# Token stacks by whole 128x128 transposes, with a new order of the mixer's instructions

## Chip, core and metric

One core of a Trainium2 chip. The metric is the device time of one launch in microseconds (us); the median of a few runs counts.

## What is computed

A decoder trunk of two layers for 256 tokens of width 2048, in float32. Each layer is RMS norm, one input projection, three parallel mixers (HGRN2, latent attention with 8 heads, RWKV-7 with 8 heads of 64), their outputs joined and projected, a residual, then norm and a SwiGLU feed-forward. The parts that matter here, cut from the reference:

```python
# attention of one block of 128 queries
s = where(k_idx <= q_idx, (q_nope @ k_nope.T + q_rope @ k_rope.T) * scale, MASK)
p = softmax(s);  o = p @ v
# RWKV-7, per head and token
sa    = state @ -kk_t
state = state * w_t + outer(sa, kk_t * a_t) + outer(v_t, k_t)
y_t   = state @ r_t
```

## The kernel before

The weights (some 400 MB) stream through four slots of `raw`. ScalarE rounds each half slot to `w_hi` (line 450), VectorE takes the rest as `w_lo` (line 875), and TensorE does three products of 128x128 by 128x512 for each tile (lines 1447 to 1449). This fills nearly all of the time. Between the input projection and the output projection of each layer lies the mixer stretch (TensorE from line 1760 on), in which attention and RWKV-7 are worked off together. Its order is written out by hand, once for each engine: lines 688 to 772 for ScalarE, 1203 to 1320 for VectorE, the end of the GpSimd block for GpSimd, lines 1799 to 1937 for TensorE. Engines meet by semaphores only, and each works its list in order.

RWKV-7 is evaluated in chunks of 64 tokens. `rw_r`, `rw_k`, `rw_v`, `rw_a` and `rw_kk` are held as 4 pairs of heads by 256 tokens, two heads of 64 channels in the halves of the 128 partitions. 16 tiles of 64x64 for each half (`JC` = 16) stand for 4 pairs by 4 chunks (`NC` = 4).
- `q_norm` scales the query's rotary part, on which GpSimd then does six rotary steps (lines 420 to 426). `k_sums`, `k_norm`, `up`, `q_turn`, `k_turn`, `r_turn` prepare the attention's keys and queries. `up(5)` to `up(7)` are the last products of the up projection; ScalarE squares and copies them in `up_out`.
- `product(left, right)` makes 16 tiles for each half by 32 products of 64x64 (`both_heads`, line 1736). The first one, of `kk` and `a`, gives the matrix of which a unit triangular inverse is wanted. VectorE masks each product (`product(k, dst, ...)`, line 1257): `mab`, `mak_t`, `mrk_t`, `mrb_t`.
- The inverse starts on VectorE from 2x2 pairs (lines 1282, 1283 and the block transposes at line 1262). Five levels follow. For each one GpSimd masks `mab` into `rw_level` (line 434), `level_g(k)` multiplies it with `inv_t`, ScalarE evicts that (`gt_out`, line 685), `level_x(k)` multiplies with `inv`, and VectorE's `level(k)` subtracts and turns (lines 1270, 1262), each in two halves.
- `stack(z, bank)` brings the tokens of `v`, `a` and `k` onto the partitions, chunk by chunk, by 32 products of 64x64 with the unit matrix; ScalarE evicts the result in one piece (`stacked`, line 671) to `v_st`, `b_st`, `k_st`.
- `attend(p)` makes the scores of a pair of heads, `score_max(p)` on VectorE adds the mask (line 1173), takes maxima (line 1176) and two small products (line 1180), `softmax(p)` on ScalarE the exponentials, `probs(p)` on VectorE scales by the inverse sums in two instructions (line 1192), `p_turn(p)` turns them, `probs_out(p)` evicts them, `mix(hf)` multiplies with the values; `mix_out` and `mix_lo` split the result for the output projection.
- In the recurrence TensorE goes over the four chunks (lines 1905 to 1937) with small products (`each`, line 1889), VectorE scales the right side (line 1313) and the state (line 1317), ScalarE copies `sa` (line 770).

PSUM has eight banks; `stack` of `v` and `a` uses 0 and 1, the products 2 and 3, later 4 to 7.

Of the kernel before, what the change touches and what calls it, by code (L numbers as in the profile page):

```python
# [35 lines left out]
P = 128  # L36
D = 2048
SEQ = 256
TT = SEQ // P
# [14 lines left out]
RC = 64  # L54
# [58 lines left out]
def build(nc, stream, x_in, positions, params, consts, lora, gains, rows, out):  # L113
    with ExitStack() as ctx:
# [237 lines left out]
        def _(pool):  # L352
# [24 lines left out]
            for l in range(DEPTH):  # L377
# [53 lines left out]
                for k in range(len(RW_LEVELS)):  # L431
                    if k:
                        pool.wait_ge(S("rw_gt_mm"), 10 * l + 2 * k)
                    tt(rw_level, mab, lev_lo[:, k, :].unsqueeze(1).broadcast_to([P, JC, RC]), ALU.mult).then_inc(
                        S("rw_level_ready"), 1)
# [4 lines left out]
        def _(act):  # L440
# [66 lines left out]
            for l in range(DEPTH):  # L507
# [160 lines left out]
                def stacked(k, dst, b0):  # L668

                    act.wait_ge(S("rw_stack_mm"), 3 * l + k + 1)  # L670
                    nc.scalar.activation(dst.rearrange("p n f -> p (n f)"), bank(b0, 2), ACT.Copy).then_inc(
                        S("rw_stacked"), 1)
# [62 lines left out]
                nc.scalar.activation(srw[:, 48:64], srw[:, 32:48], ACT.Exp, scale=-C0).then_inc(S("rw_half_decay"), 1)  # L735
                up_out(5)
                q_out(1)
                k_std(0)
                stacked(0, v_st, 0)
# [15 lines left out]
                softmax(3)  # L755
# [4 lines left out]
                probs_out(3)  # L760
                mix_out(0)
                gt_out(3)
                mix_out(1)
# [3 lines left out]
                stacked(2, k_st, 6)  # L767
# [76 lines left out]
        def _(dve):  # L844
# [108 lines left out]
            for l in range(DEPTH):  # L953
# [216 lines left out]
                def score_max(p):  # L1170
# [3 lines left out]
                       "mla_s_read", 4 * l + p + 1)  # L1174
                    for off, cols, n in parts:
# [8 lines left out]
                def probs(p):  # L1184
# [5 lines left out]
                    for off, cols, n in parts:  # L1190
                        z = scores[:, h2, cols]
                        u(tt(z, z, along(small[:, 64 + off + 2 * p:66 + off + 2 * p], n), MUL))  # L1192
# [46 lines left out]
                dve.sem_inc(S("rw_v_ready"), 1)  # L1239
                v(tt(rw_a, rw_a, rw_kk, MUL))  # L1240
                q_norm()
                dve.wait_ge(S("rw_exp"), 3 * l + 1)
                v(tt(rw_r, rw_r, rw_e_r, MUL))
                k_sums(0)
                dve.wait_ge(S("rw_exp"), 3 * l + 2)
                v(tt(rw_kk, rw_kk, rw_e_kk, MUL))
                k_norm(0)
                dve.wait_ge(S("rw_bonus_mm"), ev)
                v(tt(rw_bonus.rearrange(flat), bank(2, 2), rw_v.rearrange(flat), MUL))
                dve.wait_ge(S("rw_exp"), 3 * ev)  # L1250
                vs(tt(rw_a, rw_a, rw_e_b, MUL), "rw_b_done", ev)
                vs(tt(rw_k, rw_k, rw_e_b, MUL), "rw_ab_done", ev)
                k_sums(1)

# [26 lines left out]
                product(1, mab, 2, "strict_lo")  # L1281
                v(tt(inv, mab, over(C("pair_lo"), JC, RC), MUL))
# [3 lines left out]
                dve.sem_inc(S("rw_xt"), 1)  # L1286
                k_norm(1)
                dve.wait_ge(S("rw_half_decay"), ev)
                hd = srw[:, 48:64].rearrange("p (j c) -> p j c", j=4)
                md = srw[:, 64:80].rearrange("p (j c) -> p j c", j=4)  # L1290
                v(tt(md[:, :, 0:3], hd[:, :, 0:3], hd[:, :, 1:4], MUL))
                score_max(0)
                level(0)
                score_max(1)
                probs(0)
                score_max(2)
                probs(1)
                score_max(3)
                level(1)
                probs(2)  # L1300
                probs(3)
                level(2)
                mix_lo(0)
                mix_lo(1)
                product(2, mak_t, 4, "strict_up")
                level(3)
                product(3, mrk_t, 6, "incl_up")
                product(4, mrb_t, 4, "incl_up")
# [119 lines left out]
        def _(pe):  # L1428
# [81 lines left out]
            for l in range(DEPTH):  # L1510
# [245 lines left out]
                def unit_of(hp, n):  # L1756
                    return idst[hp, :]

                def stack(z, b0):
                    both_heads(b0, range(JC), chunk_of(z), unit_of, RC).then_inc(S("rw_stack_mm"), 1)  # L1760
# [347 lines left out]
```

## Time and profile before

| | us |
|---|---|
| median of 3 runs (2363.12 to 2363.3) | 2363.16 |
| profiled run | 2363.51 |
| its span, first to last instruction | 2361.7 |
| TensorE busy | 2329.8 (99%) |
| VectorE busy | 1331.0 (56%) |
| ScalarE busy | 1090.3 (46%) |
| GpSimd busy | 60.6 (3%) |

A matmul's busy time overlaps with the next one's, so the start of one row to the start of the next is its cost. In a chain of waits each step goes back to what released it. An instruction's row also holds time in which it has begun but is held up.

### The profile page before, as it was taken

To read this page: it belongs to the slowest core of one execution; us is meant where nothing else is said; L and a number is where in the kernel's file an instruction comes from. 1 tells how busy PE (TensorE), PEld (TensorE's weight loads), DVE (VectorE), ACT (ScalarE), POOL (GpSimd) and SP (SyncE) were. 2 spreads that over 40 slices of the span, in tenths; PEclk is the share of its full clock that TensorE was granted. 3 is DMA by queue.
4 is the path that set the end of the run, shared out by engine and by line. 5 is a ranking of instruction groups with operands and counts; after the bars stand their busy time and mean duration, and the time that the engine had idled before them with its cause. 6 is when DMAs were issued, how large, how long until landed. Compare 5 with 4: busy or idle time off the path is not lost.

```text
span 2361.7 us, 34240 instructions
## 1 busy us (share of the span) xinstructions
PE 2329.8 (99%) x13929; PEld 1931.9 (82%) x13929; DVE 1331.0 (56%) x1402; ACT 1090.3 (46%) x1336; POOL 60.6 (3%) x60
## 2 busy tenths in 40 slices
PE   8999999999999999999999999999999999999999
PEld 7888688888888888888888886888888888888887
DVE  5686676544545445455556857665454554454444
ACT  6554644444443344444445546455444433444443
POOL 0000210000000000000000002100000000000000
PEclk9999999999999999999999999999999999999999
DMA  7453304555555555555554532045555555555553
GB/s 297 165 185 134 115 18 164 193 181 194 191 182 196 192 190 189 195 183 191 186 189 152 196 113 102 21 165 190 183 192 195 179 195 196 192 185 193 189 187 141
DMA packets 59523, 407.11 MB, mean 172 GB/s; under 512 B 6608, under 2 KB 6704, under 8 KB 13200
## 3 DMA queue, kind: packets, MB, share of 16 engines
q1 hardware_dynamic: 58720, 401.66, 47.4%
q0 software_dynamic: 688, 3.78, 0.5%
q8 instruction: 88, 1.44, 0.2%
q14 instruction: 27, 0.22, 0.0%
HBM read 403.32 MB, written 2.10 MB: 172 GB/s over the span
## 4 chain that ended last, share of the span: by engine, by line
PE 94%; DVE 5%; issue 1%; ACT 0%; DMA 0%; DVEq 0%; SPq 0%; ACTq 0%
PE psum L1447 28%; PE psum L1449 28%; PE psum L1448 28%; PE psum L1641 2%; PE psum L1889 1%; PE psum L1736 1%; PE psum L1976 1%; PE psum L1542 1%; PE psum L1481 1%; DVE arena L1192 1%; DVE arena L1262 0%; DVE small L1176 0%; DVE arena L1173 0%; PE psum L1717 0%; DVE arena L1283 0%
## 5 line engine op out<-in xcount | busy, mean ns | idle before, releaser
L875 DVE TENSOR_TENSOR w_lo<-raw,w_hi 128x1024 fp32r<-128x1024 f32 (+2 forms) x752 | 901.5, 1205 | 848.7 <-ACT w_hi L450 841.8
L450 ACT ACTIVATE w_hi<-raw 128x1024 fp32r<-128x1024 f32 (+2 forms) x752 | 781.9, 1044 | 1082.6 <-PE psum L1449 1081.0
L1447 PE MATMUL psum<-w_hi,hT_hi 128*128 128x512 f32 (+2 forms) x2128 | 821.6, 386 | 3.1 <-DVE w_lo L875 3.1
L1449 PE MATMUL psum<-w_hi,hT_lo 128*128 128x512 f32 (+2 forms) x2128 | 816.4, 384 | 0.0
L1448 PE MATMUL psum<-w_lo,hT_hi 128*128 128x512 f32 (+2 forms) x2128 | 816.3, 384 | 0.0
L1447 PEld LDWEIGHTS psum<-w_hi,hT_hi 128*128 128x128 f32 x2128 | 399.8, 188 | 81.7 <-DVE w_lo L875 2.4
L1449 PEld LDWEIGHTS psum<-w_hi,hT_lo 128*128 128x128 f32 x2128 | 399.7, 188 | 78.3
L1448 PEld LDWEIGHTS psum<-w_lo,hT_hi 128*128 128x128 f32 x2128 | 399.9, 188 | 76.5
L1447 PE MATMUL psum<-w_hi,act_hi 128*128 128x512 f32 x872 | 340.4, 390 | 0.0
L1449 PE MATMUL psum<-w_hi,act_lo 128*128 128x512 f32 x872 | 339.4, 389 | 0.0
L1448 PE MATMUL psum<-w_lo,act_hi 128*128 128x512 f32 x872 | 339.3, 389 | 0.0
L1449 PEld LDWEIGHTS psum<-w_hi,act_lo 128*128 128x128 f32 x872 | 163.7, 188 | 34.0
L1447 PEld LDWEIGHTS psum<-w_hi,act_hi 128*128 128x128 f32 x872 | 163.7, 188 | 33.6
L1448 PEld LDWEIGHTS psum<-w_lo,act_hi 128*128 128x128 f32 x872 | 163.7, 188 | 33.6
L1641 PE MATMUL psum<-raw,arena 128*128 128x384 f32 (+1 forms) x192 | 71.8, 525 | 2.0 <-ACT arena L639 1.3
L1641 PEld LDWEIGHTS psum<-raw,arena 128*128 128x128 f32 x192 | 35.4, 190 | 31.1 <-issue 13.8
L1382 DVE TENSOR_TENSOR act_lo<-psum,act_hi 128x1024 f32 (+1 forms) x22 | 26.9, 1224 | 37.9 <-ACT act_hi L825 37.9
L887 DVE SCALAR_TENSOR_TENSOR hT_lo<-psum,gain_col,hT_hi 128x256 fp32r<-128x256 f32 x64 | 26.6, 477 | 13.7 <-ACT hT_hi L472 13.7
L1736 PE MATMUL psum<-arena 64*64 64x64 f32 x1024 | 32.4, 219 | 1.5 <-ACT arena L685 1.5
L1736 PEld LDWEIGHTS psum<-arena 64*64 64x64 f32 x1024 | 30.8, 135 | 3.4 <-ACT arena L685 1.8
L825 ACT ACTIVATE act_hi<-psum 128x1024 f32 (+1 forms) x22 | 22.6, 1027 | 20.8 <-PE psum L1976 20.8
L908 DVE TENSOR_TENSOR x<-x,psum 128x1024 f32<-128x1024 f32 x23 | 27.9, 1213 | 4.9 <-PE psum L1449 4.9
(317 smaller groups left out, 1206.9 us busy)
## 6 DMA issues: line engine op xcount, KB each, us to landing
raw<-stream_dram SPq DMA_DIRECT2D x360, 1024.0 KB, 4.8
raw<-stream_dram SPq DMA_DIRECT2D x16, 512.0 KB, 3.5
raw<-stream_dram SPq DMA_DIRECT2D x8, 768.0 KB, 4.2
raw<-stream_dram SPq DMA_DIRECT2D x8, 640.0 KB, 3.7
x<-x_in_dram SPq DMA_DIRECT2D x4, 512.0 KB, 9.2
lor<-lora_dram POOLq DMA_DIRECT2D x2, 832.0 KB, 10.6
con<-consts_dram POOLq DMA_DIRECT2D x1, 1648.0 KB, 12.1
out_dram<-x SPq DMA_DIRECT2D x3, 512.0 KB, 7.4
```

The costliest lines, as they stand in the source:

```text
L450: nc.scalar.activation(w_hi[:, q % HALF_RING, 0:2 * w], raw[:, j % 4, hf * 2 * w:(hf + 1) * 2 * w], ACT.Copy).then_inc(hi_done, 1)
L875: tt(w_lo[:, q % HALF_RING, 0:2 * w], raw[:, j % 4, hf * 2 * w:(hf + 1) * 2 * w], w_hi[:, q % HALF_RING, 0:2 * w].bitcast(F32), SUB).then_ ...
L887: last = stt(hT_lo[:, 4 * c + k, :], bank(x_turn_bank(n, c), 2)[:, k * SEQ:(k + 1) * SEQ], gain_col[:, n * KT + 4 * c + k:n * KT + 4 * c + ...
L908: vs(tt(xs, xs, psum[:, b0:b0 + 2, :], ADD), "x_added", n_added)
L1192: u(tt(z, z, along(small[:, 64 + off + 2 * p:66 + off + 2 * p], n), MUL))
L1382: tt(act_lo[:, k, :], bank(4, 2).rearrange("p (k t) -> p k t", k=4), act_hi[:, k, :].bitcast(F32), SUB).then_inc(S("act_lo_ready"), 1)
L1447: mm(o, a_hi, w_hi[:, r, cols], start=(k == 0), stop=False)
L1448: mm(o, a_hi, w_lo[:, r, cols], start=False, stop=False)
L1449: last = mm(o, a_lo, w_hi[:, r, cols], start=False, stop=(k == n_k - 1))
L1481: last = tr(bank(x_turn_bank(n, c), 2)[:, k * SEQ + t * P:k * SEQ + (t + 1) * P], x[:, t, c * CH + k * P:c * CH + (k + 1) * P], ident)
L1641: last = mm(psum[:, UP_BANK[c] + t, 0:w], src[:, k, t * P:(t + 1) * P], raw[:, c % 4, k * w:(k + 1) * w], start=(k == 0), stop=(k == nk - 1))
L1736: last = mm(bank(b0, 2)[hp, m * w:(m + 1) * w], left(hp, n), right(hp, n), start=True, stop=True)
```

## The change

`stack` now turns a whole block of 128 channels by 128 tokens with one transpose, eight in all. The result has tokens on the partitions and two heads side by side in the columns, so `stacked` puts each of the four combinations of token half and head into its place by an eviction of its own, two of which go from one half of the partitions to the other. The orders on all four engines change: the product of `kk` and `a` is ahead of `k_turn(0)`, `r_turn` and the stack of `a`; the first inverse and the mask of level 0 are taken by VectorE right from PSUM, and `mab` is written later; `score_max` is divided into `score_add` and the rest; `probs` scales in four instructions with a column of scalars; `softmax(3)`, `p_turn(3)`, `probs(3)`, `level_x(3)`, `level(3)`, the stack of `k` and the last product move. The diff, cut to its core:

```diff
     pool.wait_ge(S("rw_m_ready"), 4 * l + 1)
-    for k in range(len(RW_LEVELS)):
-        if k:
-            pool.wait_ge(S("rw_gt_mm"), 10 * l + 2 * k)
+    for k in range(1, len(RW_LEVELS)):
+        pool.wait_ge(S("rw_gt_mm"), 10 * l + 2 * k)
         tt(rw_level, mab, lev_lo[:, k, :].unsqueeze(1).broadcast_to([P, JC, RC]), ALU.mult).then_inc(
...
         act.wait_ge(S("rw_stack_mm"), 3 * l + k + 1)
-        nc.scalar.activation(dst.rearrange("p n f -> p (n f)"), bank(b0, 2), ACT.Copy).then_inc(
-            S("rw_stacked"), 1)
+        turned = bank(b0, 2).rearrange("p (m h i) -> p m h i", h=2, i=RC)
+        tiles = dst.rearrange("p (m c) i -> p m c i", c=2)
+        halves = (EVEN, ODD)
+        for h in range(2):
+            for c in range(2):
+                last = nc.scalar.activation(tiles[halves[h], :, c, :], turned[halves[c], :, h, :], ACT.Copy)
+        last.then_inc(S("rw_stacked"), 1)
...
     nc.scalar.activation(srw[:, 48:64], srw[:, 32:48], ACT.Exp, scale=-C0).then_inc(S("rw_half_decay"), 1)
+    q_out(1)
+    stacked(0, v_st, 0)
     up_out(5)
-    q_out(1)
     k_std(0)
-    stacked(0, v_st, 0)
     up_out(6)
...
     softmax(2)
-    softmax(3)
     probs_out(0)
...
     probs_out(2)
-    probs_out(3)
+    softmax(3)
     mix_out(0)
     gt_out(3)
+    probs_out(3)
     mix_out(1)
...
     gt_out(4)
-    stacked(2, k_st, 6)
+    stacked(2, k_st, 4)
     for c in range(NC):
...
-    def score_max(p):
+    def score_add(p):
         h2, b0 = slice(2 * p, 2 * p + 2), 4 + 2 * (p % 2)
...
+    def score_max(p):
+        h2 = slice(2 * p, 2 * p + 2)
         for off, cols, n in parts:
...
         settle()
-        for off, cols, n in parts:
-            z = scores[:, h2, cols]
-            u(tt(z, z, along(small[:, 64 + off + 2 * p:66 + off + 2 * p], n), MUL))
+        for h in range(2 * p, 2 * p + 2):
+            for off, cols, n in parts:
+                z = scores[:, h, cols]
+                u(ts(z, z, small[:, 64 + off + h:65 + off + h], None, MUL))
         settle()
...
         v(tt(rw_v, v_first[:, :, :], rw_v, SUB))
-    dve.sem_inc(S("rw_v_ready"), 1)
+        dve.sem_inc(S("rw_v_ready"), 1)
+    q_norm()
     v(tt(rw_a, rw_a, rw_kk, MUL))
-    q_norm()
     dve.wait_ge(S("rw_exp"), 3 * l + 1)
     v(tt(rw_r, rw_r, rw_e_r, MUL))
-    k_sums(0)
     dve.wait_ge(S("rw_exp"), 3 * l + 2)
     v(tt(rw_kk, rw_kk, rw_e_kk, MUL))
+    dve.wait_ge(S("rw_exp"), 3 * ev)
+    v(tt(rw_a, rw_a, rw_e_b, MUL))
+    k_sums(0)
+    dve.wait_ge(S("rw_bonus_mm"), ev)
+    vs(tt(rw_bonus.rearrange(flat), bank(2, 2), rw_v.rearrange(flat), MUL), "rw_bonus_done", ev)
     k_norm(0)
-    dve.wait_ge(S("rw_bonus_mm"), ev)
-    v(tt(rw_bonus.rearrange(flat), bank(2, 2), rw_v.rearrange(flat), MUL))
-    dve.wait_ge(S("rw_exp"), 3 * ev)
-    vs(tt(rw_a, rw_a, rw_e_b, MUL), "rw_b_done", ev)
-    vs(tt(rw_k, rw_k, rw_e_b, MUL), "rw_ab_done", ev)
     k_sums(1)
+    dve.wait_ge(S("rw_half_decay"), ev)
+    hd = srw[:, 48:64].rearrange("p (j c) -> p j c", j=4)
+    md = srw[:, 64:80].rearrange("p (j c) -> p j c", j=4)
+    v(tt(md[:, :, 0:3], hd[:, :, 0:3], hd[:, :, 1:4], MUL))
...
-    product(1, mab, 2, "strict_lo")
-    v(tt(inv, mab, over(C("pair_lo"), JC, RC), MUL))
+    dve.wait_ge(S("rw_m_mm"), 4 * l + 1)
+    v(tt(inv, bank(2, 2).rearrange("p (n t) -> p n t", n=JC), over(C("pair_lo"), JC, RC), MUL))
     vs(stt(inv, inv, -1.0, over(idst, JC, RC), MUL, ADD), "rw_x", 10 * l + 1)
...
     dve.sem_inc(S("rw_xt"), 1)
+    dve.wait_ge(S("mla_rope_done"), ev)
+    v(tt(rw_level, bank(2, 2).rearrange("p (n t) -> p n t", n=JC), over(lev_lo[:, 0, :], JC, RC), MUL))
+    dve.sem_inc(S("rw_level_ready"), 1)
+    vs(tt(rw_k, rw_k, rw_e_b, MUL), "rw_ab_done", ev)
     k_norm(1)
-    dve.wait_ge(S("rw_half_decay"), ev)
-    hd = srw[:, 48:64].rearrange("p (j c) -> p j c", j=4)
-    md = srw[:, 64:80].rearrange("p (j c) -> p j c", j=4)
-    v(tt(md[:, :, 0:3], hd[:, :, 0:3], hd[:, :, 1:4], MUL))
+    product(1, mab, 2, "strict_lo")
+    score_add(0)
     score_max(0)
     level(0)
+    score_add(1)
     score_max(1)
     probs(0)
+    score_add(2)
     score_max(2)
+    score_add(3)
     probs(1)
-    score_max(3)
     level(1)
     probs(2)
+    score_max(3)
+    level(2)
     probs(3)
-    level(2)
     mix_lo(0)
     mix_lo(1)
+    level(3)
     product(2, mak_t, 4, "strict_up")
-    level(3)
     product(3, mrk_t, 6, "incl_up")
-    product(4, mrb_t, 4, "incl_up")
+    product(4, mrb_t, 6, "incl_up")
     level(4)
...
-    def unit_of(hp, n):
-        return idst[hp, :]
...
     def stack(z, b0):
-        both_heads(b0, range(JC), chunk_of(z), unit_of, RC).then_inc(S("rw_stack_mm"), 1)
+        for j in range(4):
+            for t in range(TT):
+                last = tr(bank(b0, 2)[:, (TT * j + t) * P:(TT * j + t + 1) * P], z[:, j, t * P:(t + 1) * P], ident)
+        last.then_inc(S("rw_stack_mm"), 1)
...
             pe.wait_ge(S("rw_x"), 10 * l + 2 * k + hf + 1)
+            if k == 0:
+                pe.wait_ge(S("rw_m_ready"), 4 * l + 1)
             if not last:
...
     if l == 0:
-        pe.wait_ge(S("rw_v_ready"), ev)
+        pe.wait_ge(S("rw_shifted"), 4 * l + 3)
         stack(rw_v, 0)
-    up(5)
     pe.wait_ge(S("rw_rk"), ev)
...
     if l:
-        pe.wait_ge(S("rw_v_ready"), ev)
+        pe.wait_ge(S("rw_v_ready"), l)
         stack(rw_v, 0)
+    up(5)
     up(6)
     up(7)
+    pe.wait_ge(S("rw_bonus_done"), ev)
+    product(rw_kk, rw_a, 2)
     k_turn(0)
-    pe.wait_ge(S("rw_b_done"), ev)
-    product(rw_kk, rw_a, 2)
+    r_turn(range(4))
+    r_turn([4])
     pe.wait_ge(S("rw_stacked"), 3 * l + 1)
     stack(rw_a, 0)
-    r_turn(range(4))
-    r_turn([4])
     attend(0)
...
     level_g(2)
+    p_turn(2)
     level_x(2)
-    p_turn(2)
-    p_turn(3)
     mix(0)
     level_g(3)
+    p_turn(3)
+    level_x(3)
     mix(1)
...
     product(rw_k, rw_kk, 4)
-    level_x(3)
+    level_g(4)
     pe.wait_ge(S("mla_mix_lo"), 2 * ev)
     product(rw_k, rw_r, 6)
-    level_g(4)
     pe.wait_ge(S("rw_m_ready"), 4 * l + 2)
-    product(rw_a, rw_r, 4)
+    stack(rw_k, 4)
     pe.wait_ge(S("rw_m_ready"), 4 * l + 3)
-    stack(rw_k, 6)
+    product(rw_a, rw_r, 6)
     level_x(4)
...
         if c == 0:
-            pe.wait_ge(S("rw_stacked"), 3 * ev)
+            pe.wait_ge(S("rw_m_ready"), 4 * ev)
+            each(6, 0, stacked(mrk_t, 0), stacked(v_st, 0), first=True)
             pe.wait_ge(S("rw_xt"), 12 * ev)
-        if c < NC - 1:
+        elif c < NC - 1:
             each(2, 0, stacked(k_st, c), stacked(v_st, c), first=True)
-            if c:
-                each(2, 0, unit, old)
+            each(2, 0, unit, old)
         pe.wait_ge(S("rw_rhs_ready"), NC * l + c + 1)
...
         if c == 0:
-            pe.wait_ge(S("rw_m_ready"), 4 * ev)
-        each(6, 256 * c, stacked(mrk_t, c), stacked(v_st, c), first=True)
-        if c:
+            pe.wait_ge(S("rw_stacked"), 3 * ev)
+            each(2, 0, stacked(k_st, 0), stacked(v_st, 0), first=True)
+        else:
+            each(6, 256 * c, stacked(mrk_t, c), stacked(v_st, c), first=True)
             each(6, 256 * c, in_chunk(rw_r, c), old)
...
```

## Rows read from the trace of the kernel before

**Rows 1.** Page, part 4: the chain that ended last, by engine.
```profile
PE 94%; DVE 5%; issue 1%; ACT 0%; DMA 0%; DVEq 0%; SPq 0%; ACTq 0%
```

**Rows 2.** Three stretches: busy us (instructions) by engine, granted clock, DMA share, GB/s.
```profile
270.00:360.00 90.00, 80.68 (x1718) 67.95 (x1720) 67.22 (x94) 44.49 (x81) 23.24 (x11) 1.00 0.16 60
...
1445.00:1535.00 90.00, 81.38 (x1734) 68.54 (x1736) 70.23 (x95) 44.76 (x82) 24.11 (x11) 1.00 0.17 61
...
360.00:420.00 60.00, 60.00 (x355) 49.97 (x352) 40.23 (x44) 29.63 (x36) 2.80 (x7) 1.00 0.52 180
```

**Rows 3.** Timeline, TensorE, layer 0: start, us, instruction, count [idle before <- releaser].
```profile
270.68 2.08 PE L1736 MATMUL psum<-con,arena 64*64 64x64 f32 x64 [1.45 <-DVEq L1239]
...
286.35 1.04 PE L1661 MATMUL psum<-con,arena 128*128 128x128 f32 x8
...
328.63 0.70 PE L1717 MATMUL psum<-arena 128*128 128x256 f32 x2
...
345.58 0.68 PE L1889 MATMUL psum<-arena 64*64 64x64 f32 x16
```

**Rows 4.** Timeline, TensorE, layer 1.
```profile
1445.42 3.67 PE L1641 MATMUL psum<-raw,arena 128*128 128x512 f32 x8 [0.77 <-issue]
...
1519.98 0.68 PE L1889 MATMUL psum<-arena 64*64 64x64 f32 x16
```

**Rows 5.** Timeline, VectorE, layer 0.
```profile
270.97 1.22 DVE L1240 TENSOR_TENSOR arena<-arena 128x1024 f32<-128x1024 f32 x1 [0.60 <-DVE arena L1233]
...
278.38 1.78 DVE L1246 TENSOR_TENSOR arena<-arena 128x1024 f32<-128x1024 f32 x1
...
283.90 2.15 DVE L1251 TENSOR_TENSOR arena<-arena 128x1024 f32<-128x1024 f32 x1
...
289.52 1.23 DVE L1257 TENSOR_TENSOR arena<-psum,con 128x1024 f32<-128x1024 f32 x1 [0.95 <-PE psum L1736]
...
292.04 3.26 DVE L1283 SCALAR_TENSOR_TENSOR arena<-arena,con 128x1024 f32<-128x1024 f32 x1
...
299.70 1.01 DVE L1176 TENSOR_REDUCE small<-arena 128x2 f32<-128x256 f32 x2
300.75 0.75 DVE L1180 SCALAR_TENSOR_TENSOR small<-small 128x2 f32<-128x2 f32 x2
...
315.27 0.69 DVE L1270 TENSOR_TENSOR arena<-arena,psum 128x512 f32<-128x512 f32 x1
...
318.47 3.18 DVE L1192 TENSOR_TENSOR arena<-arena,small 128x256 f32<-128x256 f32 x2
```

**Rows 6.** Timeline, VectorE, layer 1.
```profile
1452.37 2.15 DVE L1246 TENSOR_TENSOR arena<-arena 128x1024 f32<-128x1024 f32 x1
...
1460.31 2.19 DVE L1252 TENSOR_TENSOR arena<-arena 128x1024 f32<-128x1024 f32 x1
...
1489.38 0.69 DVE L1270 TENSOR_TENSOR arena<-arena,psum 128x512 f32<-128x512 f32 x1
```

**Rows 7.** Timeline, GpSimd, layer 0.
```profile
290.82 3.39 POOL L434 TENSOR_TENSOR gain<-arena,con 128x1024 f32<-128x1024 f32 x1 [5.85 <-DVE arena L1257]
299.05 2.36 POOL L434 TENSOR_TENSOR gain<-arena,con 128x1024 f32<-128x1024 f32 x1 [4.83 <-PE psum L1736]
...
318.73 2.38 POOL L434 TENSOR_TENSOR gain<-arena,con 128x1024 f32<-128x1024 f32 x1 [7.54 <-PE psum L1736]
```

**Rows 8.** Timeline, GpSimd, layer 1, the last rotary step.
```profile
1459.27 2.13 POOL L426 TENSOR_TENSOR arena<-arena 128x512 f32<-128x512 f32 x1
```

**Rows 9.** Timeline, VectorE, layer 0, scalings with one tensor.
```profile
188.65 0.48 DVE L1108 TENSOR_SCALAR arena<-arena,small 128x512 f32<-128x512 f32 x1
189.04 0.35 DVE L1109 TENSOR_SCALAR arena<-arena,small 128x256 f32<-128x256 f32 x1
189.31 0.25 DVE L1110 TENSOR_SCALAR arena<-arena,small 128x64 f32<-128x64 f32 x1
```

**Rows 10.** Timeline, ScalarE, layer 0, two evictions of 512 columns.
```profile
318.74 1.06 ACT L685 ACTIVATE arena<-psum 128x512 f32<-128x512 f32 x2
```

## Prediction

> **What bounds it now.** The chain of waits is 94% TensorE and 5% VectorE [rows 1]. Outside the mixers TensorE is never idle (60.00 of 60.00 us in the stretch behind the first one), so time can come out there only by fewer products, and the change has none there. In the mixer stretches, 90 us per layer, it works 80.68 and 81.38 us with VectorE at 67.22 and 70.23 and a clock of 1.00 [rows 2]. What decides inside them is read next from TensorE in order of time [rows 3, 4]: `stack` by 32 small products takes 2.08 us, eight whole transposes take 1.04 us. Then VectorE in order of time [rows 5, 6] beside GpSimd [rows 7, 8]: VectorE runs nearly without a gap, and some of its instructions take far longer than others of their shape.
>
> **Whom GpSimd holds.** The two-tensor instruction of the first inverse (line 1283) takes 3.26 us [rows 5] while GpSimd's mask of level 0 runs from 290.82 to 294.21; it ends 1.1 us after that [rows 7]. The second scaling of `probs(2)` waits likewise: 3.18 us for the pair, beside a GpSimd mask from 318.73 to 321.11 [rows 5, 7]. GpSimd waits in its turn (3.39 us against 2.38 for the same mask). In layer 1 they alternate, 2.1 us an instruction on either side [rows 6, 8]. A maximum over one tensor keeps 1.01 us for two while a mask runs [rows 5]. So instructions with two SBUF tensors are held, reductions are not.
>
> I follow one chain per layer through three points: C, VectorE's start of `level(1)` (315.27 and 1489.38), D, TensorE's `mix(1)` (328.63), and E, the first product with `inv_t` (345.58 and 1519.98) [rows 3 to 6]. Behind E both kernels do the same.
>
> **Up to C, layer 0.** The chain begins on VectorE behind `rw_rk` (270.38: 0.6 before the row at 270.97). What goes:
> - its four gaps, the first of 0.60 and the last of 0.95 us [rows 5], 4.0 together. The squares of `up(5)` come earlier, because `stack(rw_v)` no longer waits for `rw_v_ready` (1.45 us idle [rows 3]) and is 1 us shorter, and `k_sums(0)` now stands four multiplications later; the product has `kk` and `a` before the key turning. I leave 0.2.
> - the holds: 0.56 and 0.93 at two multiplications (1.78 and 2.15 us where an unheld one takes 1.22), 2.03 (line 1283: level 0 is now masked by VectorE from PSUM, so GpSimd is silent there), 0.52 and 0.58 at the two small ones at line 1180, 4.6 together.
> - `score_max(3)` without its addition goes behind C: 1.4.
>
> What comes:
> - `r`, `kk` and `a` are now multiplied directly behind `q_norm`, just while GpSimd does its six rotary steps. By the alternation of [rows 6, 8] three of four are held for 0.95 each: 2.8. The multiplication in `k_norm(0)` meets the last rotary step: 0.9. The small one behind the mask of level 1 waits 0.4. 4.1 together.
> - the mask of level 0, 1.26 and its signal 0.15: 1.4. The mask into `mab` stays, only later.
> - the four scalings of `probs` instead of two: single-tensor ones start 0.39, 0.27 and some 0.16 us behind one another for 512, 256 and 64 columns [rows 9], so 0.2, 0.27, 0.2 and 0.35 to the end, 1.0; the two of before take 1.0 unheld. Nothing.
>
> C comes at 315.3 − 4.0 − 4.6 − 1.4 + 0.2 + 4.1 + 1.4 = 311.0: 4.3 early. TensorE has to follow: `product(kk, a)` at 283.1 behind `up(7)`, `k_turn(0)` 285.5, `attend(0)` 289.2, `level_g(0)` 292.5, `level_x(0)` 296.6 (it waits for `mab`), `level_g(1)` 303.3, `p_turn(1)` 311.0. Its work is early everywhere, so VectorE leads.
>
> ScalarE's evictions of a stack in four go from 1.0 to about 2.0 us (two of 512 columns: 1.06 [rows 10]; a quarter has 512 columns in 64 partitions). `stacked(0)` holds up `up_out(5)`, which has 2 us to spare against `k_sums(0)`; `stacked(1)` ends at 291.1, before `level_g(0)`; `stacked(2)` is 4 us early. A price of nothing up to 1 us a quarter would cost 0 to 0.6 us per layer; I take nothing, nearest to the row.
>
> **Layer 1.** No gaps to win: VectorE had none. Its holds were 3.5 in four multiplications (first and last in [rows 6]), 2.0 at line 1283 and 0.9 at line 1180, 6.5 in all; the same 4.1 come. C: 6.5 − 4.1 = 2.4 early. `up(5)`, which now stands behind the bonus and the stack, filled the time until `rw_v_ready` (it began at 1445.42 [rows 4]); TensorE now idles some 0.3 there and 0.9 before the product, which waits for `rw_bonus_done`. That is off the chain.
>
> **C to D: 13.4 before.** Now `p_turn(2)` must wait for `probs(2)` (C + 4.4, unheld), then come 0.76 for it, `level_x(2)` 1.96, `mix(0)` 2.65, `level_g(3)` 2.0, `p_turn(3)` 0.76 and `level_x(3)` 1.96: 14.5. Lost: 1.1. The two inverse steps stood partly behind D before.
>
> **D to E: 16.95 before [rows 3].** The output of `mix(1)` is split by VectorE at D + 5.3, as before; then `level(3)`, formerly behind `product(2)` but with TensorE busy beside it. Its second half is turned at D + 7.5, `level_g(4)` ends at 8.2, `product(k, r)` 10.2, its mask 11.6; the stack of `k`, 1 us instead of 1.96, is hidden under this mask; `product(a, r)` 13.7, its mask 15.1, `level(4)` 17.0, right side and first `inv_t` product 17.7. Lost: 0.75. The bound of these signals and of GpSimd's claims is 1 us per layer either way.
>
> **Sum.** Layer 0: 4.3 − 1.1 − 0.75 = 2.45. Layer 1: 2.4 − 1.1 − 0.75, and 0.3 since its C to E was 30.6 rather than 30.3: 0.85. Together 3.3. The profiled run took 2363.5 (span 2361.7, 1.8 around it), so 2360.2; the median is 0.35 below its profiled run: **2359.9**. Six stacks save 5.8 us of TensorE work; the rest becomes waiting.
>
> **Rivals.**
> - **The scalings are held by GpSimd too.** For it: 256 columns more cost such a scaling 0.12 us [rows 9], half of what 1.22 us for 1024 columns of a two-tensor one gives, so it may read through both inputs at once. Against: the unheld reductions with one tensor [rows 5]. In `probs(2)` the mask starts 3.46 us behind C (318.73 − 315.27), the scalings lie at 3.2 to 4.2: the last two would wait for its end, 2.05 more, and `p_turn(2)` with them, ahead of which nothing is left for TensorE. 2 × 2.05: 2364.0.
> - **Held twice, slower.** Given that, `probs(0)` decides: its last scaling starts at 305.53, GpSimd takes the inputs for level 2 at about 305.6 (`level_g(1)` 303.3 + 2.08 + 0.25). If the mask is 0.1 us earlier relative to it, 2.1 more per layer on VectorE's chain: 2368.2.
> - **The front is not held.** If GpSimd's rotary steps yield to VectorE or end earlier, 2.8 + 0.9 go, of which TensorE (`up(7)`, 283.1) lets 1.5 through in layer 0 and 2.5 in layer 1: 2355.9. For it: GpSimd too is seen waiting; against: the alternation.
>
> The Trainium skill speaks for the first rival: its page GPSIMD Engine Reference, section "Key points", says that GpSimd shares its SBUF interfaces with VectorE and contends with instructions in a 2-port mode or with two SBUF inputs, and VectorE: DVE Perf Modes, "Mode 2×_2P", that a float32 scaling in SBUF uses both ports. The trace agrees for two inputs; no row shows the other. By it the time is 2364.0.
>
> **Chances.** Forecast 0.40, first rival 0.25, held twice 0.12, front not held 0.18, else 0.05. The 8-in-10 range leaves out the second rival and what is else and puts the 2 us of unknown costs half on the outer cases: 2355.5 to 2366; the forecast's own is 2358 to 2362. A measurement can tell about 0.2%, 4.7 us: faster than 2358.4 is the third rival and a tail of the forecast, 0.25; slower than 2367.9 is the second rival's greater part, 0.10; within, 0.65.
>
> **What the profile would show.** Stack transposes of 1 us; VectorE without gaps from 270 to C at 311 and 1487; its multiplications at 2.1 us beside GpSimd's rotary steps; no 3 us at the inverse; about 1 us idle before `p_turn(2)` and 1 us between the halves of `level_g(4)`. Scalings of `probs(2)` over 3 us prove the first rival; a C later than 313 the second; multiplications at 1.2 us the third. Wrong altogether: quarters of a stack over 1 us, or TensorE waiting for them.

## The result, and the profile after

The changed kernel takes 2368.61 us (median of 11 runs, 2366.95 to 2370.66), the kernel before 2363.30 in the same comparison: a ratio of 1.0022, interval 1.0013 to 1.003. It is slower by 5.3 us, where 3.4 less were forecast, and above the range. Its profiled run took 2367.03 us, its span is 2365.2.

The page of the changed kernel has the same chain, nearly all TensorE, as [rows 1]:

```profile
span 2365.2 us, 33610 instructions
...
PE 93%; DVE 5%; issue 0%; ACT 0%; DMA 0%; SPq 0%; DVEq 0%; ACTq 0%
```

Timeline of the changed kernel, TensorE, layer 0, then layer 1 (start, us, instruction, count, idle before and releaser). It answers to [rows 3, 4]; line 1725 is `p_turn`, 1752 a product of 64x64 tiles, 1775 a stack, 1733 `mix`, 1761 `level_g(4)` and `level_x(4)`, 1907 the recurrence.

```profile
283.82 2.08 PE L1752 MATMUL psum<-arena 64*64 64x64 f32 x64
...
288.47 1.04 PE L1775 MATMUL psum<-con,arena 128*128 128x128 f32 x8
...
317.38 0.87 PE L1725 MATMUL psum<-con,arena 128*128 128x128 f32 x6 [3.04 <-DVEq L1202]
318.18 3.34 PE L1752 MATMUL psum<-arena 64*64 64x64 f32 x64
...
329.37 0.70 PE L1733 MATMUL psum<-arena 128*128 128x256 f32 x2
...
335.57 0.69 PE L1761 MATMUL psum<-arena,gain 32*32 32x32 f32 x32 [1.30 <-DVE arena L1281]
336.95 0.69 PE L1761 MATMUL psum<-arena,gain 32*32 32x32 f32 x32 [0.68 <-DVE arena L1281]
...
347.51 0.68 PE L1907 MATMUL psum<-arena 64*64 64x64 f32 x16 [2.17 <-DVE arena L1329]
```

```profile
1493.89 1.54 PE L1725 MATMUL psum<-con,arena 128*128 128x128 f32 x6 [3.04 <-DVEq L1202]
1495.37 3.68 PE L1752 MATMUL psum<-arena 64*64 64x64 f32 x64
...
1506.93 0.70 PE L1733 MATMUL psum<-arena 128*128 128x256 f32 x2
...
1524.72 0.68 PE L1907 MATMUL psum<-arena 64*64 64x64 f32 x16 [1.82 <-DVE arena L1329]
```

Read the third row first: TensorE stands idle for 3.04 us ahead of `p_turn(2)`, in both layers, and the products behind it take 3.34 and 3.68 us where the same 64 products take 2.08 elsewhere. Nothing like either stands in [rows 3, 4].

Timeline of the changed kernel, VectorE, layer 0, one row of layer 1, then GpSimd and ScalarE, layer 0. They answer to [rows 5, 6], [rows 7] and [rows 10]; line 1251 is a multiplication, 1294 the first inverse, 1200 the scalings, 1281 a level, 433 GpSimd's mask, 675 the quarters of a stack.

```profile
274.14 2.18 DVE L1251 TENSOR_TENSOR arena<-arena 128x1024 f32<-128x1024 f32 x1
...
288.49 1.22 DVE L1294 SCALAR_TENSOR_TENSOR arena<-arena,con 128x1024 f32<-128x1024 f32 x1
...
305.00 1.01 DVE L1200 TENSOR_SCALAR arena<-arena,small 128x128 f32<-128x128 f32 x4
...
310.98 0.69 DVE L1281 TENSOR_TENSOR arena<-arena,psum 128x512 f32<-128x512 f32 x1
...
314.17 3.09 DVE L1200 TENSOR_SCALAR arena<-arena,small 128x128 f32<-128x128 f32 x4
```

```profile
1487.49 0.69 DVE L1281 TENSOR_TENSOR arena<-arena,psum 128x512 f32<-128x512 f32 x1
```

```profile
305.76 2.46 POOL L433 TENSOR_TENSOR gain<-arena,con 128x1024 f32<-128x1024 f32 x1 [6.62 <-PE psum L1752]
...
314.42 2.49 POOL L433 TENSOR_TENSOR gain<-arena,con 128x1024 f32<-128x1024 f32 x1 [6.20 <-PE psum L1752]
```

```profile
276.21 2.39 ACT L675 ACTIVATE gain<-psum 64x512 f32<-64x512 f32 x4
```

C is at 310.98, as forecast. The four scalings of `probs(0)` take 1.01 us: the last of them starts at 305.65 us, 0.11 ahead of GpSimd's mask. The same four of `probs(2)` take 3.09, beside the mask from 314.42 to 316.91.

Windows of the changed kernel, two in layer 0 and three in layer 1: the stretch, its length, busy us (instructions) of TensorE, its weight loads, VectorE, ScalarE and GpSimd, the granted clock, DMA share, GB/s.

```profile
314.00:318.00 4.00, 0.96 (x18) 0.82 (x14) 3.82 (x8) 0.60 (x1) 2.49 (x1) 1.00 0.02 4
318.00:322.00 4.00, 4.00 (x68) 3.66 (x67) 2.42 (x6) 2.93 (x9) 0.00 (x0) 0.58 0.00 0
...
1490.00:1494.00 4.00, 0.96 (x31) 0.82 (x28) 3.79 (x8) 0.70 (x2) 2.49 (x1) 0.85 0.00 0
1494.00:1498.00 4.00, 4.00 (x56) 3.67 (x58) 1.78 (x5) 2.53 (x8) 0.00 (x0) 0.50 0.02 4
1498.00:1502.00 4.00, 4.00 (x36) 3.59 (x33) 3.42 (x10) 0.40 (x2) 0.00 (x0) 0.79 0.00 0
```

With the 3 us of waiting the granted clock falls to 0.50, the 1.2 GHz level of the two: by these windows for about 3.4 us in layer 0 and 6.9 in layer 1, where it begins before the wait is over. The mean clock of the run, which was 1.000 or 0.999 before, is 0.998 in the 2 runs at 2367.0, 0.997 in those between 2368.0 and 2368.6 and 0.996 in those from 2369.5. The spread of the new kernel from run to run goes with its clock.

**Where the time went, span against span.** In layer 0, E minus C is 347.51 − 310.98 = 36.5 where 14.5 + 17.7 = 32.2 were forecast; in layer 1 it is 1524.72 − 1487.49 = 37.2, where 30.6 + 1.55 = 32.15 were.

| us, against the forecast | layer 0 | layer 1 |
|---|---|---|
| C | 0.0 | −0.3 |
| scalings held (3.09 − 1.01) | +2.1 | +2.1 |
| slow products behind the wait | +1.5 | +2.6 |
| D to E (18.14 and 17.79; 17.7 forecast) | +0.4 | +0.1 |
| C to D, the rest | +0.3 | +0.3 |
| behind E, "both the same" | −1.1 | −1.2 |

That is 6.8, and −3.3 + 6.8 = 3.5 = 2365.2 − 2361.7. The slow products are, in layer 0, `level_x(2)` 3.27 from start to start where 2.01 is full speed, and 0.27 at `mix(0)`; in layer 1, `p_turn(2)` 1.48 where 0.80 is, `level_x(2)` 3.60, and 0.3 at `mix(0)`. The rest of C to D lies in the six steps from `p_turn(2)` to `level_x(3)`: at full speed they take 0.80, 2.01, 2.82, 2.01, 0.81 and 2.01 us (`mix(0)` put at what `mix(1)` takes), 10.46 where 10.09 was forecast. "Behind E" is the first product of the output projection: it comes 0.8 late in layer 0 (361.76 for 360.96) though E is 1.9 late.

### The profile page after: what moved, and what is told of

It reads as the page before. It is cut to its first block, busy times and chain, and to the rows that moved or that the text cites. A ratio compares the mean times of both kernels' runs of the same rounds, so it can differ in the third digit from the quotient of the medians.

```text
span 2365.2 us, 33610 instructions
## 1 busy us (share of the span) xinstructions
PE 2329.6 (98%) x13593; PEld 1929.6 (82%) x13593; DVE 1330.2 (56%) x1420; ACT 1098.7 (46%) x1354; POOL 55.3 (2%) x58
## 4 chain that ended last, share of the span: by engine, by line
PE 93%; DVE 5%; issue 0%; ACT 0%; DMA 0%; SPq 0%; DVEq 0%; ACTq 0%
PE psum L1463 28%; PE psum L1465 28%; PE psum L1464 28%; PE psum L1657 2%; PE psum L1907 1%; PE psum L1752 1%; PE psum L1995 1%; PE psum L1558 1%; PE psum L1497 1%; DVE arena L1200 0%; DVE arena L1273 0%; DVE arena L1281 0%; PE psum L1733 0%; DMA x<-x_in_dram 0%; DVE arena L1177 0%
```

## The experiments

The first theory: GpSimd's mask of level 3 holds the scalings of `probs(2)`; TensorE waits 2 us longer, and the wait brings its clock down. The rivals: the scalings' own form is slow; the evictions in quarters, or the new stacks, cost the time; the clock falls for another reason; the tail of the new order is slow in itself. Each run stands beside runs of the kernel before, with medians of 2363.3 to 2363.7.

**The mask of level 3 by VectorE, behind `probs(2)`.**

```diff
-    for k in range(1, len(RW_LEVELS)):          # GpSimd
+    for k in (1, 2, 4):
...
     probs(2)                                    # VectorE
+    dve.wait_ge(S("rw_level_ready"), 5 * l + 3)
+    dve.wait_ge(S("rw_gt_mm"), 10 * l + 6)
+    tt(rw_level, mab, over(lev_lo[:, 3, :], JC, RC), MUL).then_inc(S("rw_level_ready"), 1)
```

> The changed kernel, with the mask of level 3 taken by VectorE behind probs(2) instead of by GpSimd, which is then silent while the scalings of probs(2) run. Theory (the scalings are held by GpSimd, and the 3.0 us of idle TensorE that follow let its clock fall): the four scalings take 1.0 us instead of 3.09, p_turn(2) starts some 4.5 us behind the start of level(1) instead of 6.4, the idle time before it is 1.1 us, level_x(2) takes 2.0 us instead of 3.3 and 3.6, the granted clock is 1.000; per layer 2.1 + 1.3 to 2.5 us less, so 2360 to 2361. Rival (the scalings are slow for their own sake, or the loss lies in the evictions and the tail): scalings stay above 2 us or the time above 2365.

2360.63 us (2359.71 to 2364.97), ratio 0.999, interval 0.998 to 0.9999: 8.0 less than the changed kernel. Its timeline, VectorE, then TensorE, layer 0:

```profile
314.04 1.01 DVE L1202 TENSOR_SCALAR arena<-arena,small 128x128 f32<-128x128 f32 x4
```

```profile
315.16 0.88 PE L1730 MATMUL psum<-con,arena 128*128 128x128 f32 x6 [0.96 <-DVEq L1204]
315.96 2.08 PE L1757 MATMUL psum<-arena 64*64 64x64 f32 x64
...
333.82 3.62 PE L1757 MATMUL psum<-arena 64*64 64x64 f32 x64
```

Without a GpSimd mask beside them the same four instructions take 1.01 us, and TensorE waits 0.96 us, which is the forecast's "about 1 us idle". So GpSimd was the cause of the hold. The time is as expected, the clock is not: it was to be 1.000, and it is 0.999 in seven runs and 0.996 in the two of 2365 us. In the profiled run (0.998) the product behind `level_g(4)` takes 3.62 us.

**The old two-tensor scalings in the new kernel.**

```diff
-        for h in range(2 * p, 2 * p + 2):
-            for off, cols, n in parts:
-                z = scores[:, h, cols]
-                u(ts(z, z, small[:, 64 + off + h:65 + off + h], None, MUL))
+        for off, cols, n in parts:
+            z = scores[:, h2, cols]
+            u(tt(z, z, along(small[:, 64 + off + 2 * p:66 + off + 2 * p], n), MUL))
```

> The changed kernel, with the scalings of probs as before: two instructions with two tensors each instead of four with a column of scalars. Theory (GpSimd holds both kinds alike): the pair in probs(2) takes 3.1 to 3.2 us, as the four took 3.09, everything else is the same: 2367 to 2370. Rival (single-tensor scalings are held less, so that the edit is worth something where a mask meets them): 2 us or more slower than the changed kernel.

2368.74 us (2366.9 to 2369.52), ratio 1.002, interval 1.0011 to 1.003: no difference from the changed kernel. Its timeline, VectorE and GpSimd, layer 0:

```profile
313.98 3.17 DVE L1199 TENSOR_TENSOR arena<-arena,small 128x256 f32<-128x256 f32 x2
```

```profile
314.23 2.37 POOL L433 TENSOR_TENSOR gain<-arena,con 128x1024 f32<-128x1024 f32 x1 [6.21 <-PE psum L1751]
```

TensorE, layer 0:

```profile
317.26 1.54 PE L1724 MATMUL psum<-con,arena 128*128 128x128 f32 x6 [3.12 <-DVEq L1201]
...
337.41 3.51 PE L1751 MATMUL psum<-arena 64*64 64x64 f32 x64
```

3.17 us for two instructions with two tensors, 3.09 for four with one: both kinds are held until about the end of the mask. The edit of `probs` is worth nothing either way.

The last row shows a second thing. This kernel has the waits of the changed one (3.12 us, then 1.30 and 0.68 at `level_g(4)`), but its profiled run (2369.16 us, clock 0.996) has more slow stretches than that of the changed kernel (2367.03, 0.998): the product behind `level_g(4)` is slow too, and from 346 to 350 us, where the recurrence begins, the clock is 0.74. The same waits are followed by a fall in one profile and not in the other.

TensorE has nothing to do between `level_g(2)` and `p_turn(2)`'s wait for `probs(2)`. The next run changes that.

**`level_x(2)` ahead of `p_turn(2)`**, so that the wait is shorter while the hold stays.

```diff
-    p_turn(2)
     level_x(2)
+    p_turn(2)
```

> The changed kernel, with level_x(2) ahead of p_turn(2) on TensorE as in the kernel before. Theory: the hold stays (3.09 us), but level_x(2) fills the wait; p_turn(2) starts at the same 6.4 us behind the start of level(1), mix(0) some 8.3 us behind it instead of 10.5 and 11.5, and with no idle stretch above 1 us the clock stays at 1.000: 2.4 and 3.4 us less, 2361 to 2362. Rival (the clock falls for the share of small products in the stretch and not for the 3 us of idle): clock still 0.996 to 0.998, and not below 2364.

2366.23 us (2362.54 to 2368.06), ratio 1.0009, interval 1.0 to 1.0019, clock 0.996 to 0.999: 4 to 5 us over what I expected, and where the rival was put (the share of small products); the kernel with `level(3)` ahead and `level_x(2)` first, below, speaks against that rival. Its timeline, TensorE, layer 0:

```profile
317.21 0.87 PE L1725 MATMUL psum<-con,arena 128*128 128x128 f32 x6 [1.19 <-DVEq L1202]
...
335.03 3.38 PE L1752 MATMUL psum<-arena 64*64 64x64 f32 x64
```

The wait is 1.19 us instead of 3.04 and `level_x(2)` is no longer slow. But the product behind `level_g(4)` is, as with the mask on VectorE, and in layer 1 the clock is 0.63 from 1494 to 1498 us, behind the wait of 1.19 and one of 0.90 ahead of `mix(0)`. So a shorter wait is not enough.

**The wait filled with work that nobody needs**, at the same place: once by 20 transposes, once by 10 products in float32.

```diff
     level_g(2)
+    pe.wait_ge(S("rw_x"), 10 * l + 6)
+    for _ in range(20):
+        tr(bank(2)[:, 0:P], ident, ident)
```

> The changed kernel, with 20 transposes of the unit matrix (some 2.4 us, into a PSUM bank that is free then) in the wait before p_turn(2); nothing depends on them. It adds nothing but TensorE's work. Theory (idle TensorE lets the clock fall): the hold stays, p_turn(2) starts when it did, level_x(2) takes 2.0 us, clock 1.000, 1.5 and 2.3 us less: 2363 to 2363.5 with a spread below 1 us. Rival (transposes are no work in the clock's eyes, so it falls all the same): level_x(2) 3.3 us, the time of the changed kernel, 2367 to 2370.

> As the run with transposes, with 10 products of 128x128 by 128x128 in float32 (some 2.1 to 2.4 us) in their place. Theory: as there, 2363 to 2363.5. If products count for the clock and transposes don't, this one alone is 4 us faster than the changed kernel. Rival (the clock falls for another reason): both stay at 2367 to 2370.

Transposes: 2366.55 us (2365.34 to 2370.73), ratio 1.0015, interval 1.0005 to 1.0024. Products: 2367.06 (2364.53 to 2369.49), ratio 1.0016, interval 1.0006 to 1.0025. Both miss by 3 us and are alike. In both, `level_x(2)` is back at 2.08 us and the product behind `level_g(4)` slow (3.68 and 3.49). Timeline of the kernel with transposes, TensorE, layer 0:

```profile
318.09 2.08 PE L1752 MATMUL psum<-arena 64*64 64x64 f32 x64
...
336.31 3.68 PE L1752 MATMUL psum<-arena 64*64 64x64 f32 x64
```

So at least two places bring the clock down: the wait for `probs(2)`, and `level_g(4)`, whose halves wait 1.30 and 0.68 us for VectorE (rows above), because `mix_lo(1)` stands ahead of `level(3)`. Covering one leaves the other. That is tested next.

**`level(3)` ahead of `mix_lo(1)`, the hold left in.**

```diff
     mix_lo(0)
+    level(3)
     mix_lo(1)
-    level(3)
```

> The changed kernel, with level(3) ahead of mix_lo(1) on VectorE, so that level_g(4) need not wait for the output of mix(1). The hold in probs(2) and the 3.0 us before p_turn(2) stay. Theory (two stretches of idle TensorE cost clock, each by itself, and the tail costs its own 2 us): the 1.3 and 0.7 us of idle at level_g(4) go, 2.0 us per layer, 4 together; the clock still falls behind the 3.0 us before p_turn(2): 2364 to 2365, clock 0.997 to 0.998. Rival (the tail is bound by the masks of the last products anyway): less than 1.5 us together, not below 2367.

2364.95 us (2363.68 to 2365.14), ratio 1.0005, interval 0.9995 to 1.0014: 3.7 less than the changed kernel, of which the removed waits (1.30 + 0.68, twice) can account for all. The clock is 0.996 in eight of ten runs, a little below the 0.997 to 0.998 expected. Timeline of this kernel, TensorE, layer 0: the two halves are one group, without a wait.

```profile
319.09 3.68 PE L1752 MATMUL psum<-arena 64*64 64x64 f32 x64
...
335.42 1.20 PE L1761 MATMUL psum<-arena,gain 32*32 32x32 f32 x64
```

**The same, with the 20 transposes in the wait for `probs(2)`.** The two kernels differ in nothing but useless work.

> The changed kernel with level(3) ahead of mix_lo(1), and 20 idle transposes in the wait before p_turn(2), on which nothing depends. The hold and all starts up to p_turn(2) stay as in the kernel with level(3) first alone (2364.95, clock 0.996). Theory (idle stretches alone): level_x(2) takes 2.0 us, clock 0.999 to 1.000, and the difference is the price of the clock alone: 2360 to 2362. Rival (transposes don't keep it up once the tail is closed): clock 0.996 to 0.997, 2364 to 2365.

2361.45 us (2360.33 to 2362.71), ratio 0.9988, interval 0.9978 to 0.9997; the slowest of these runs is faster than the fastest without the transposes (2363.68). One window of the kernel without the transposes, then of the one with them, layer 0:

```profile
318.00:322.00 4.00, 4.00 (x60) 3.67 (x60) 1.75 (x6) 2.81 (x9) 0.00 (x0) 0.50 0.00 0
```

```profile
318.00:322.00 4.00, 4.00 (x77) 3.77 (x77) 3.17 (x7) 2.93 (x9) 0.00 (x0) 1.00 0.02 4
```

Added work makes the kernel 3.5 us faster, the granted clock 1.00 instead of 0.50, and 77 instructions are worked off where 60 were. Measured against each one's own runs of the kernel before, the difference is 3.9. This is the price of the fall at this one place, in both layers: the hold is in both kernels (3.09 and 3.13 us), and both profiles also have a fall at the start of each recurrence (0.64 and 0.66 in windows of 4 us without the transposes, 0.75 and 0.59 with them), which the transposes do not touch.

**`level(3)` and `level_x(2)` first, the hold left in.**

> The changed kernel with level(3) ahead of mix_lo(1) and level_x(2) ahead of p_turn(2). The hold in probs(2) stays (3.09 us). Theory (idle stretches alone bring the clock down): the longest idle stretches are 1.2 us before p_turn(2) and 1.8 to 2.2 before the first product with inv_t, the clock is 0.999 to 1.000, the time 2 x 2.0 below the kernel with level_x(2) first less its lost clock: 2358 to 2360, spread 2 us. Rival (the kind of work counts): clock 0.997 or lower, 2361 or more.

2359.88 us (2358.11 to 2360.78), ratio 0.9982, interval 0.9972 to 0.9991: held scalings and all, it is below both kernels. The time is as expected; the clock, 0.998 in seven of ten runs, lies between what the theory and the rival asked for. In layer 0 it falls behind waits of 1.19 and 0.90 us, at `mix(0)`:

```profile
318.00:322.00 4.00, 3.10 (x12) 2.54 (x11) 3.68 (x9) 2.92 (x9) 0.00 (x0) 0.68 0.00 0
```

**`level(3)` first and the mask of level 3 by VectorE**, and then `level_x(2)` first as well.

> The changed kernel with both edits: the mask of level 3 by VectorE, and level(3) ahead of mix_lo(1). Theory: no hold, no idle stretch of TensorE above 1.9 us (the one before the first product with inv_t), clock 0.999 to 1.000; 2 x 2.2 us below the run with the mask alone, less its lost clock: 2355 to 2357, with a spread of 1.5 us. It would then be faster than the kernel before by 0.3%. Rival (the clock falls for the remaining waits before the recurrence): clock 0.998, 2358 to 2361.

> The kernel with level(3) first and the mask of level 3 by VectorE, and level_x(2) ahead of p_turn(2) as well. Theory (without the hold the order of these two hardly matters: 1.0 us idle before p_turn(2) against 0.7 before level_x(2)): within 1 us of it, 2354 to 2356. Rival (the order of the two was half of the loss): 2352 or less.

2354.98 us (2354.01 to 2356.86), ratio 0.9963, interval 0.9951 to 0.9976, clock 0.999 to 1.000; with `level_x(2)` first 2355.65 (2353.43 to 2356.16), no more. With the hold gone, 1 us of waiting is left, and moving `level_x(2)` into it gives nothing that can be measured.

**The two halves of the change apart.** The new stacks and their evictions with the orders of before, then the orders of the change with the old stacks.

```diff
-        both_heads(b0, range(JC), chunk_of(z), unit_of, RC).then_inc(S("rw_stack_mm"), 1)
+        for j in range(4):
+            for t in range(TT):
+                last = tr(bank(b0, 2)[:, (TT * j + t) * P:(TT * j + t + 1) * P], z[:, j, t * P:(t + 1) * P], ident)
+        last.then_inc(S("rw_stack_mm"), 1)
```

> The kernel before, with the stacks by whole transposes and their evictions in four pieces, and nothing else of the change: all orders as before. Theory (the stacks themselves are sound, the order loses): TensorE does each stack 1 us quicker, but VectorE's chain decides, so it gains 0 to 3 us, 2360.5 to 2363.5, clock 1.000. Rival (the evictions of 2.4 us instead of 1.0 hold TensorE up, or transposes let the clock fall): 2365 or more.

> The changed kernel with the stacks as before (32 products and one eviction), its orders kept. Theory: three stacks of 1 us more per layer on TensorE, of which those of v and a lie beside VectorE's chain and that of k is hidden under a mask; the evictions are 1.4 us shorter, which ends the wait of level_g(0) for them (0.7 us, beside VectorE's chain): the same as the changed kernel within 1.5 us, 2367 to 2370. Rival (the saved transposes are worth their 5.8 us): 2373 or more.

New stacks alone: 2359.66 us (2359.28 to 2361.07), ratio 0.9986, interval 0.9976 to 0.9995. New orders alone: 2371.78 (2368.99 to 2373.9), ratio 1.0031, interval 1.0019 to 1.0044. So the stacks bring 3.6 us and the orders as written lose 8.5. Of the rivals, the quarters of an eviction are cleared: they take about 2.4 us instead of 1.0 and the kernel is faster nonetheless.

**The new stacks, the old orders, and the mask of level 3 by VectorE behind `probs(3)`.** The kernel before is held too, at the second scaling [rows 5]; this frees it, for a fair comparison of the orders.

> The orders of before, with the new stacks, and the mask of level 3 taken by VectorE behind probs(3). It tells what the new order is worth once it is free of hold and tail: the kernel with both edits took 2355.0. Theory: the hold in probs(2) goes (2.1 us, of which TensorE, busy with level_x(2), lets 1 us through): 2357 to 2358.5, so the new order is worth 2 to 3 us. Rival (the new order is worth nothing): 2355 or less.

2357.45 us (2357.15 to 2359.1), ratio 0.9975, interval 0.9964 to 0.9985, clock 1.000 or 0.999. Against 2354.98 the new order, with `level(3)` first, is worth 2.5 us where neither is held (2.2 if each is measured against its own runs of the kernel before).

**`q_norm` behind the four multiplications**, in the best kernel so far. This tests the front: there the forecast let GpSimd's rotary steps hold three of four.

```diff
-    q_norm()
     v(tt(rw_a, rw_a, rw_kk, MUL))
...
     v(tt(rw_a, rw_a, rw_e_b, MUL))
+    q_norm()
```

> The kernel with level(3) first and the mask of level 3 by VectorE, and q_norm behind the multiplication of a by its decay, so that GpSimd's rotary steps don't run beside the four multiplications. Theory (three of the four are held for 0.95 us each, as in the profile of the changed kernel): they take 1.23 us each, the chain up to the first inverse is 1.3 us shorter in layer 0, where TensorE's up(7) bounds it, and 2 in layer 1; 2351 to 2353. Rival (the holds move to k_norm(0) and the inverse, or r_turn waits for the rotary steps): no gain, 2354 to 2356.

2352.74 us (2352.55 to 2353.99), ratio 0.9954, interval 0.9938 to 0.9971: 10.8 below the kernel before in the same comparison, 2.2 below the best so far, and the fastest found. Its timeline, VectorE, layer 0:

```profile
274.45 1.23 DVE L1254 TENSOR_TENSOR arena<-arena 128x1024 f32<-128x1024 f32 x1
275.71 1.23 DVE L1256 TENSOR_TENSOR arena<-arena 128x1024 f32<-128x1024 f32 x1
```

A multiplication that takes 2.18 us beside GpSimd's rotary steps takes 1.23 without them.

## Why the prediction was wrong

**Right.** The chain through C, D and E, and the whole of the front. C was forecast at 311.0 and 2.4 us early, and came at 310.98 and, layer 1 having begun 0.8 late, 2.7 early. TensorE followed within 0.7 us (product 283.82 for 283.1). The multiplications were held at 2.2 us and the first inverse was not (1.22); the run with `q_norm` later shows that the first is GpSimd's doing. "About 1 us idle before `p_turn(2)`" is right for scalings that are not held: 0.96 with the mask on VectorE. D to E was 18.1 and 17.8 where 17.7 was forecast.

**The step that failed: "`p_turn(2)` must wait for `probs(2)` (C + 4.4, unheld)".** It came at C + 6.40 in both layers, because the four scalings were held for 2.1 us, 4.2 for the two layers. The word "unheld" rests on the same reading as the "nothing" for "the four scalings of `probs` instead of two": I put the single-tensor form beside the unheld maxima of [rows 5] and against the rule. Up to C the "nothing" came true (1.01 us each for `probs(0)` and `probs(1)`), but there no scaling started while a mask ran. With the mask taken away the scalings of `probs(2)` take 1.01 too, with the old form in their place 3.17, so it is GpSimd that holds them and the form makes no difference. This is the first rival, its mechanism and its size (2.05 forecast). The Trainium skill was right here: GPSIMD Engine Reference, "Key points", has GpSimd contend with VectorE instructions in a 2-port mode, and VectorE: DVE Perf Modes, "Mode 2×_2P", counts a float32 scaling in SBUF among these; the 3.09 beside the mask against 1.01 agrees. The maxima were the wrong neighbour: near in operand count, but not the same kind of instruction.

**The term that was missing: TensorE's clock.** The sum took 1.00 from [rows 2] and priced every wait at its own length. The wait for `probs(2)` was put at 1 us and turned out 3.04, and the clock fell to 0.5 for about 3.4 us in layer 0 and 6.9 in layer 1, which costs 1.5 and 2.6 us in the profiled run. The pair of kernels that differ in 20 transposes alone prices it at 3.5. The median run lies another 1.6 us above the profiled one, at a lower mean clock (0.997 for 0.998). It has no trace; that its clock falls at more places, as in the profile with the old scalings, fits but is not shown. 2359.9 + 4.2 is 2364.1, so the first rival as I wrote it (2364.0) is also too low: it kept the mechanism and left out what it sets off. The remaining 4.5 to 2368.6 are the slow products, 4.1 by the table, 1.6 by which the median run lies above the profiled one and 0.3 by which it was forecast below it, and 1.1 of D to E and the rest of C to D, less the 2.6 gained at C of layer 1 and behind E.

**The tail, right in size and not seen as a danger.** D to E was to lose 0.75, with "1 us between the halves of `level_g(4)`"; they wait 1.30 and 0.68. I took this as the price of the order and did not ask whether the order could do without it: `level(3)` ahead of `mix_lo(1)` gives 3.7 with the hold and 5.6 without (2360.63 to 2354.98). It is also a second place at which the clock falls.

**The second rival had the time and not the mechanism.** It gave 2368.2, close to 2368.6, by a second hold at `probs(0)`. The rows refute it: those scalings take 1.01 us, and C is not late. But it was close, as the rival had said: the last scaling started 0.11 us ahead of the mask in both layers (305.65 for 305.76, 1482.16 for 1482.27). In its place stands the clock. The third rival, an unheld front, is refuted by the 2.18 us rows.

**Small ones.** A quarter of a stack takes 0.6 us, 2.39 for four where 2.0 was forecast; TensorE waits for it once per layer, 0.66 and 0.76 us ahead of `level_g(0)`. That was named as a sign of being wrong altogether; the sign came and meant nothing, for `level_x(0)` waits for VectorE's `mab` anyway (0.31 us), and the kernel with the old stacks is no faster. Layer 1 begins 0.8 late because layer 0 ends so. "Behind E both kernels do the same" holds for the work and not for the time: the stretch is 1.1 and 1.2 us shorter. Most of this is a wait in the recurrence of before, 0.81 us in layer 0 and 0.90 in layer 1, which the trace puts down to issue and which is absent after. Why it is absent was not tried. Timeline of the kernel before, TensorE, layer 0:

```profile
357.33 1.02 PE L1889 MATMUL psum<-arena 64*64 64x64 f32 x26 [0.81 <-issue]
```

**What stays open.** Why the clock falls with some of these waits and not with others. With the same program, the kernel with only the mask moved had a mean clock of 0.996 in two runs (2365 us) and of 0.999 in seven (2359.7 to 2361.5). The length of the wait does not decide it alone: the clock fell behind 1.19 and 0.90 us in the two kernels with `level_x(2)` first, and at the start of the recurrence, behind a wait of 1.8 to 2.2 us, in some profiles and not in that of the changed kernel (2.17 us, clock 1.00). The kernel before waits 1.30 us at `level_g(2)`, then 0.23, 0.74, 0.31 and 0.56, at a clock of 1.00 all through. Timeline of the kernel before, TensorE, layer 0:

```profile
316.11 1.15 PE L1736 MATMUL psum<-arena,gain 64*64 64x64 f32 x32 [1.30 <-DVE arena L1270]
317.48 1.15 PE L1736 MATMUL psum<-arena,gain 64*64 64x64 f32 x32 [0.23 <-DVE arena L1270]
319.38 2.08 PE L1736 MATMUL psum<-arena 64*64 64x64 f32 x64 [0.74 <-ACT arena L685]
```

The runs show which waits to remove, not a rule by which to foresee a fall.

## What to carry to other kernels

A wait of TensorE is not priced by its length alone: where a reordering puts 3 us of idle time in one place, or 1.3 and 0.7 us around a short piece, count on slow products behind it as a possible cost (3.5 us here for one place in two layers), and look for the next such wait before filling the first. For every VectorE instruction between two TensorE steps ask what GpSimd does meanwhile; a single-tensor scaling in SBUF is held like a two-tensor one, and two cures worked: giving the GpSimd instruction beside it to VectorE, just behind the work that is waited for (8.0 us), or leaving the hold in and moving two calls, one of them TensorE work into the wait (8.7 us). Test the halves of a change apart: here the new stacks won 3.6 us and the order written for them lost 8.5, until one call of it was moved and one mask given to VectorE, after which it won 2.5 over the old one with the same mask moved.

## What was not expected of the hardware

Work of no use can pay: 20 transposes in a 3 us wait made a kernel 3.5 us faster, and transposes kept the granted clock at 1.00 (window above) as well as 10 products of float32 did (2366.55 and 2367.06 us in the same place). Where the fall at one wait was prevented, one came at a later wait, at `level_g(4)` in four kernels; the profile with the old scalings has both, so the first does not stand in for the second. Copying a 512-column quarter from 64 partitions of PSUM costs ScalarE 0.60 us (2.39 for four), so a stack in four quarters takes over twice the 1.06 of two evictions of 128 partitions [rows 10].
